# The end of a mixer: one conv tile before the reciprocal, output banks emptied between two roundings, attention tiles first

## The reference

```python
r = x + 0.5 * rms_norm(swiglu_ffn(rms_norm(x, norm_ffn1_pre), w_ffn1_gate_up, w_ffn1_down), norm_ffn1_post)
z = rms_norm(r, norm_mix_pre) @ w_in               # q | k | v | b | c | xv
attn_out = attend(q, k, v, attn_sinks)             # 8 heads, window of chunks of 64, 512 wide
conv_out = b * causal_conv3(c * xv)                # 512 wide
mixed = concat([rms_norm(attn_out, norm_attn_out), rms_norm(conv_out, norm_conv_out)]) @ w_out
r = r + rms_norm(mixed, norm_mix_post)
r = r + 0.5 * rms_norm(swiglu_ffn(rms_norm(r, norm_ffn2_pre), w_ffn2_gate_up, w_ffn2_down), norm_ffn2_post)
gate = sigmoid(rms_norm(r, norm_ple_pre) @ w_ple_gate)
r = r + rms_norm(gate * (p @ w_ple_proj), norm_ple_post)
```

## Time and profile before

| | |
|---|---|
| median of 3 runs | 1093.67 us (1092.20 to 1093.82) |
| the profiled execution's own time | 1093.74 us |
| its span | 1091.9 us |
| mean granted TensorE clock | 0.987 |
| TensorE busy | 1043.2 us (96%) |
| VectorE busy | 700.8 us (64%) |
| ScalarE busy | 509.6 us (47%) |
| GpSimd busy | 288.6 us (26%) |

### The profile page before, as it was taken

One profiled execution on the slowest core, in us unless ns is written; L12 is line 12 of the kernel. 1 busy time (PEld: TensorE's weight loads), 2 busy tenths in 40 slices (PEclk: granted clock), 3 DMA queues, 4 the chain that ended last, 5 costly groups with the idle time before them and its releaser, 6 DMA issues.

```text
span 1091.9 us, 20075 instructions
## 1 busy us (share of the span) xinstructions
PE 1043.2 (96%) x8095; PEld 1017.4 (93%) x8095; DVE 700.8 (64%) x1057; ACT 509.6 (47%) x927; POOL 288.6 (26%) x222
## 2 busy tenths in 40 slices
PE   5999999999999999999989899899999999999896
PEld 4999999999999998888979889899999999999796
DVE  5898777776511278577782889877777651127833
ACT  4545555555422254434453554555555542226653
POOL 4113443431211132000322411434343121113311
PEclk8999999999999999999989999999999999999999
DMA  7223342435323323213222221434243532333002
GB/s 221 67 71 88 106 117 79 115 94 144 100 64 102 77 46 98 56 46 79 59 59 79 78 77 40 111 84 116 81 113 100 138 106 62 99 97 94 25 1 83
DMA packets 182678, 94.76 MB, mean 87 GB/s; under 512 B 11768, under 2 KB 180928, under 8 KB 182592
## 3 DMA queue, kind: packets, MB, share of 16 engines
q1 hardware_dynamic: 182576, 93.56, 30.9%
q10 hardware_dynamic: 16, 0.00, 0.0%
HBM read 91.15 MB, written 2.50 MB: 86 GB/s over the span
## 4 chain that ended last, share of the span: by engine, by line
PE 77%; DVE 15%; ACT 3%; issue 2%; POOL 1%; DMA 1%; DVEq 0%; SPq 0%; ACTq 0%; POOLq 0%
PE bank L1640 12%; PE bank L1642 12%; PE bank L1641 12%; PE bank L1750 9%; PE bank L1753 9%; PE bank L1752 9%; PE bank L1675 3%; PE misc L1804 2%; PE misc L1750 2%; PE misc L1753 2%; PE misc L1752 2%; DVE w_split L1070 1%; DVE x_lo L1100 1%; DVE r L1091 1%; DVE w_up L1070 1%
## 5 line engine op out<-in xcount | busy, mean ns | idle before, releaser
L1642 PE MATMUL bank<-h_hi,w_split 128*128 128x272 f32 x704 | 203.8, 290 | 0.0
L1640 PE MATMUL bank<-h_hi,w_split 128*128 128x272 f32 x704 | 203.0, 288 | 0.0
L1641 PE MATMUL bank<-h_lo,w_split 128*128 128x272 f32 x704 | 202.2, 287 | 0.0
L1070 DVE TENSOR_TENSOR w_split<-raw,w_split 128x1408 fp32r<-128x1408 f32 (+2 forms) x66 | 98.2, 1500 | 154.1 <-ACT w_split L638 154.1
L570 POOL TENSOR_TENSOR ssq<-ssq,sq 128x272 f32<-128x272 f32 x112 | 108.5, 968 | 237.2 <-ACT sq L643 226.7
L1641 PEld LDWEIGHTS bank<-h_lo,w_split 128*128 128x128 f32 x704 | 132.6, 188 | 0.1
L1640 PEld LDWEIGHTS bank<-h_hi,w_split 128*128 128x128 f32 x704 | 132.4, 188 | 0.1
L1642 PEld LDWEIGHTS bank<-h_hi,w_split 128*128 128x128 f32 x704 | 132.3, 188 | 0.0
L1750 PE MATMUL bank<-t_hi,even_blocks 128*128 128x272 f32 x432 | 126.0, 292 | 6.6 <-issue 3.8
L1753 PE MATMUL bank<-t_hi,even_blocks 128*128 128x272 f32 x432 | 125.4, 290 | 0.0
L1752 PE MATMUL bank<-t_lo,even_blocks 128*128 128x272 f32 x432 | 124.8, 289 | 0.0
(11 more groups left out here) (243 smaller groups left out, 2628.4 us busy)
## 6 DMA issues: line engine op xcount, KB each, us to landing
raw_up<-w_ffn_gate_up SPq DMA_DIRECT2D x88, 512.0 KB, 4.9
raw<-w_ffn_down SPq DMA_DIRECT2D x32, 704.0 KB, 4.9
raw<-w_in SPq DMA_DIRECT2D x14, 512.0 KB, 4.3
raw<-w_ple_gate SPq DMA_DIRECT2D x8, 512.0 KB, 3.8
x_tok<-x_prompt SPq DMA_DIRECT2D x4, 512.0 KB, 5.3
raw<-w_in SPq DMA_DIRECT2D x8, 256.0 KB, 3.8
raw<-w_out SPq DMA_DIRECT2D x16, 128.0 KB, 3.4
raw<-w_out SPq DMA_DIRECT2D x8, 256.0 KB, 3.6
```

What stands on the lines that cost most here:

```text
L1070: nc.vector.tensor_tensor(chunk_part(c, 1), chunk_raw(c), chunk_part(c, 0).bitcast(F32), ALU.subtract).then_inc(lo_made, 1)
L1640: nc.tensor.matmul(psum(u), wh, hi, start=(k == 0), stop=False)
L1641: nc.tensor.matmul(psum(u), wh, lo, start=False, stop=False)
L1642: mm = nc.tensor.matmul(psum(u), wl, hi, start=False, stop=(k == n - 1))
```

## The change

Three things are written in another order; no instruction is added or taken away but for a register operation or so.

1. *The last tile of half A before the reciprocal.* On VectorE `mix_scale(0)` moves from unit 32 to unit 33, so that unit 33 (b3, half A) is evacuated ahead of it; `mix_los(0)` moves behind the split of weight chunks 2 and 3, and `mix_scale(3)` ahead of `mix_los(2)`. On ScalarE the squares of b2 and b3 come ahead of `mix_his(0)`, and the split of weight chunk 3 ahead of `mix_his(1)`.
2. *Banks emptied between the roundings.* On ScalarE both last roots come first, then banks 0 and 1 of out's half A are emptied, then `mix_his(2)`, then banks 2 and 3, then `mix_his(3)`.
3. *Attention tiles first.* On TensorE half B of out's first group runs tiles 0 to 3 for units 0 and 1, then for units 2 and 3, and only then tiles 4 to 7 for all four. In half A the sum of group 3 moves from tile 6 of the first pair to tile 4 of unit 2, and units 2 and 3 are made one after the other.

```diff
--- before.py
+++ after.py
@@ -959,30 +959,32 @@
                     mix_squares(2 * KA, 3 * KA)
                 if v == 32:
                     mix_root(0)
-                    mix_his(0)
                 if v == 33:
                     mix_squares(3 * KA, 3 * KA + 2)
+                    mix_his(0)
                 if v == 34:
                     mix_root(1)
                     split_hi(c0 + 20)
                     mix_squares(3 * KA + 2, 3 * KA + 3)
+                    split_hi(c0 + 21)
                 if v == 35:
                     mix_his(1)
                     mix_squares(3 * KA + 3, 3 * KA + 4)
-                    split_hi(c0 + 21)
             act.wait_ge(conv_turned, 1)
             nc.scalar.activation(conv_new[:], bT[0:4 * KA, 0:P], ACT.Copy).then_inc(conv_out, 1)
             mix_root(2)
-            mix_his(2)
             mix_root(3)
-            mix_his(3)
 
 
             def out_evacuate(i, h, m):
                 number = SQ0["out"] + (4 * h + m if i == 0 else 8 + OUT_SQUARES.index(("y", h, m)))
                 evacuate(U0["out"] + 8 * i + 4 * h + m, half(y_out, 4 * i + m, h), number)
 
-            group(C0["out"], lambda h, j: (out_evacuate(0, h, 2 * j), out_evacuate(0, h, 2 * j + 1)))
+            out_evacuate(0, A, 0), out_evacuate(0, A, 1)
+            mix_his(2)
+            out_evacuate(0, A, 2), out_evacuate(0, A, 3)
+            mix_his(3)
+            second_half(C0["out"], lambda h, j: (out_evacuate(0, h, 2 * j), out_evacuate(0, h, 2 * j + 1)))
             c1, squares = C0["out"] + 2 * SLOTS, SQ0["out"] + 8
             for m in range(4):
                 out_evacuate(1, A, m)
@@ -1545,19 +1547,15 @@
                     attention_out(d - 2)
                 if 0 <= d < NTASK:
                     softmax_scale(d)
-                if v == 32:
+                if v == 33:
                     mix_scale(0)
-                if v == 33:
-                    mix_los(0)
                 if v == 34:
                     mix_scale(1)
             split_lo(c0 + 20)
             split_lo(c0 + 21)
-            mix_los(1)
-            mix_scale(2)
-            mix_los(2)
-            mix_scale(3)
-            mix_los(3)
+            mix_los(0), mix_los(1)
+            mix_scale(2), mix_scale(3)
+            mix_los(2), mix_los(3)
 
 
             second_half(C0["out"])
@@ -1941,9 +1939,17 @@
                 i, h, pos = v // 8, v % 8 // 4, v % 4
                 if i == 0 and pos == 0:
                     units = [(U0["out"] + w, C0["out"] + w % 4, lambda w=w: out_ready(w)) for w in range(v, v + 4)]
-                    hooks = {6: lambda: all_sums(SUM0["mix"] + 3)} if h == A else {}
-                    hi_pass(units[0:2], m_high, h, lambda k: pe.wait_ge(m_hi_made, 8 * h + k + 1), hooks)
-                    hi_pass(units[2:4], m_high, h, lambda k: None)
+                    def arrived(k):
+                        pe.wait_ge(m_hi_made, 8 * h + k + 1)
+                    if h == A:
+                        hi_pass(units[0:2], m_high, A, arrived)
+                        hi_pass(units[2:3], m_high, A, lambda k: None, {4: lambda: all_sums(SUM0["mix"] + 3)})
+                        hi_pass(units[3:4], m_high, A, lambda k: None)
+                    else:
+
+                        hi_pass(units[0:2], m_high, B, arrived, {}, range(0, KA))
+                        hi_pass(units[2:4], m_high, B, lambda k: None, {}, range(0, KA))
+                        hi_pass(units, m_high, B, arrived, {}, range(KA, KD))
                     for n, (u, c, _) in enumerate(units):
                         lo_pass(u, c, lambda k, h: half(m_lo, k, h), h, None if n else lambda k: pe.wait_ge(
                             m_ready, 8 * h + k + 1))
```

## The result

The changed kernel takes 1086.82 us (median of 4 runs, 1085.66 to 1087.30) beside 1093.27 us for the kernel before (4 runs): ratio 0.9937, 95% interval 0.9925 to 0.9949. The profiled execution took 1087.30 us, of which 1085.5 are its span. Two later measurements of the same program gave ratios of 0.9928 (0.9914 to 0.9941) and 0.9924 (0.9910 to 0.9937).

A forecast was written before the change was run, and what follows sets the result against it. TensorE was taken as the bound (77% of the chain), losing 7.99 us to two waits and the low clock behind them. Less 7.99 plus a new wait of 0.3 gave -7.7, from 1093.74 to 1086.0 us, range 1084.5 to 1088.6.

The forecast's parts named there:

- First wait: TensorE at the sum ahead of unit 35: wait 2.89 us, slow sum 0.43, slow unit 35 1.23; 4.55 us back.
- New wait for the weights of unit 2: TensorE at units 2 and 3 of out's half A waits for chunk 2's low part: 0.3 us, between 0 and 1.2.
- Rival 1: VectorE's full queue makes chunk 2's low part 2.3 us late and the clock falls: gain 4.6, 1089.1 us; 8%.
- Second wait: TensorE ahead of out's half B, waiting for half A's banks to be emptied: 2.38 us back.
- High pass of B: Out's half B, 64 matmuls: 9.51 us after the clock's fall against 8.45 without; 1.06 us back.
- the rule weighed in the prediction: Full-clock matmul follows after N/2.4 + 2.5 ns, 115.8 ns for 272; would give about 9.3 us, 1084.7; not adopted.
- Moves along: Out's second column group and the second FFN, released by TensorE's units or slots they free, shift with the gain.
- rival 4: TensorE's gained time is spent waiting at the second FFN's entry for something that doesn't move: 1093.7 us; 4%.
- Rival 2: Only one wait goes, TensorE still standing in half A or B: 4.55 or 3.44 come back, 1089.2 to 1090.3; 7%.
- The third sum and the tiles first: Moved sum in half A: no wait, over 1 us unmoved; half B tiles first: no wait, else no margin.
- B's `m_hi`: ScalarE ends `m_hi` 3 at 566.7, the thirteenth being there at 565.4, so half B has no wait.
- Rival 3: Small waits keep the clock at 0.50 over the out stage's 192 matmuls: up to 24.4 us more, 1110; 3%.

The follow-up runs named there:

- the first experiment: Kernel before with only the mixer's end changed (half A's last tile and squares moved ahead): 1093.15 us, ratio 0.9995.
- all banks last: Changed kernel with ScalarE emptying all four banks of out's half A after both groups of `m_hi` again: 1092.52 us, ratio 0.9981.
- the first repeat: Changed kernel measured again, unedited: 1085.50 us beside 1093.81.
- the copies earlier: Changed kernel with VectorE's two copies to `conv_rows` ahead of the last mixer weight's low part: 1085.09 us, ratio 0.9923.

## Why the prediction was right

The forecast was 1086.0 us, within 1084.5 to 1088.6; the measured medians of the changed kernel are 1086.82, 1085.50 and 1085.87. By its steps:

- *First wait.* Forecast 4.55 us back. Measured from unit 33's last matmul to the start of the out projection: 11.36 before (543.43 to 554.79), 7.47 after (543.79 to 551.26), 3.89 back; this is the largest error of the sum. The wait itself went as worked out: square at 545.21, added by 546.50, asked at 547.54. What the walk missed is 0.50 us ahead of the transposition of `conv_rows` (543.79 to 544.41 instead of 543.43 to 543.56) and a first matmul of unit 35 that holds the next back by 0.2.
- *New wait for the weights of unit 2.* Forecast 0.3, measured none: the high pass of half A takes 8.69 us (551.26 to 559.95) against 8.71 before. Rival 1 did not happen.
- *Second wait.* Forecast 2.38, measured 2.49: A's low pass to the start of B is 6.43 before (563.50 to 569.93) and 3.94 after (559.95 to 563.89).
- *High pass of B.* Forecast 1.06, measured 1.50: 9.51 before, 8.01 after. I took 0.132 us a matmul, A's 8.45 us over 64, for B at full clock, and B's is 0.125. What I misread is A: its pace is 0.125 too, but the first matmul behind a sum holds the next one back by 0.2 us, as in unit 35, and A has two such places. The rows show it: 40 matmuls from 551.26 to 556.49 and 24 from 556.74 to 559.95 are 5.23 and 3.21 us, and less 0.2 each they are 0.126 and 0.125 a matmul. B has no sum in it. The page cited for the rule weighed in the prediction (the Trainium skill, "TensorE: Matmul & The Clock Gate", section "Back-to-back issue gap") gives that formula for an isolated matmul; the trace lies between its 0.116 and my 0.132.
- Sum: 3.89 + 0.02 + 2.49 + 1.50 = 7.90, against the 7.99 - 0.3 of the prediction. That the total is only 0.2 off is luck: the term of the first wait was 0.66 too high, those of the new wait, the second wait and the high pass were 0.3, 0.1 and 0.4 too low.
- *Moves along.* The rest behind the stretch does, but in the first profile it was 1.14 us longer than before (509.55 against 508.41), and the program came 0.36 later to unit 33. So the profiled execution is 6.44 us faster (1093.74 to 1087.30) and not 7.90. The three ratios of the changed kernel come to 6.9, 7.9 and 8.3 us of the time before, around the stretch's 7.90. This is not rival 4, in which nothing comes back.
- *Rival 2* (only one wait goes) did not happen, but the first experiment shows what would have made it true: the first part alone brings 0.17 us, as the wait moves to the next place. My terms for the two waits add only because both parts were made.
- *The third sum and the tiles first.* Both were carried as zeros with a price if left out: over 1 us for the sum (measured 1.46), and "no margin" for the pairs (measured 1.42). On B's `m_hi` I was optimistic: the last is done at 568.5 and not 566.7, since VectorE came 0.4 us later to the weight splits, and these and the scalings ran slower beside GpSimd's additions (last section). The room that the new order leaves absorbed it.
- *Rival 3* (low clock): 1.00 from 546 to 576. It did not happen.

## What to carry to other kernels

When two waits follow each other, ask what the second is bound by before the first is priced: here the other engines' queue set when half B could start, so one and the same edit that brings TensorE there earlier was worth 0.17 us, and 2.61 us once that queue had been put in another order. In a queue that runs in order, put the work that frees a buffer between two groups of the work that fills the next, as soon as the buffer's last reader allows; putting that order back on one engine, with all else kept, cost 6 to 7 us. And where the whole time scatters by more than the effect, measure between two fixed instructions of the profile: the stretch repeated within 0.01 us where the clock did not fall inside it.

## What the runs showed of the hardware

**VectorE and GpSimd hold each other up.** With GpSimd's addition at 543.03 beside it, VectorE's pair of copies of 128x8 took 0.82 us and ended, by the start of the next row at 544.27, when the addition did (543.03 + 1.23 = 544.26); without it 0.24. The addition took 1.23 to 1.38 beside VectorE's work between SBUF tiles and 0.77 or 0.78 without. Four scalings at 565.78 took 2.07, with the second of the two additions in the row from 564.89 beside them, and 1.50 in the kernel before, with none. The Trainium skill, "SBUF — State Buffer", section "Who interferes with whom", says that the two engines share a pair of ports, that a copy can take it for a whole instruction and that an instruction with two inputs in SBUF meets GpSimd's reads. The traces agree: the first of the two copies was held for 0.58 us, and the reciprocal at 563.90, whose input is in PSUM, kept its 1.84 beside the addition at 564.89.

**The clock after a wait is not the same twice.** A wait of 2.7 or 2.3 us was followed by some 3 us at 0.50; that of 4.2 us in the first experiment by some 3, and that of 4.1 us with all banks last by about 6. The wait of 3.5 us in the second FFN was followed by none, some 3 or nearly 7 us at 0.50 in different executions of programs that are the same there; around that of 1.97 us ahead of the sum of squares behind the output projection (608.69 in the first profile of the changed kernel) it was none in the first repeat, some 3 us in the first profile, and nearly 7 with the copies earlier. The rest behind the stretch differs by 2.5 us over the twelve profiles, and the head of the program, where unit 33 was reached between 541.77 and 543.99, by 2.2. Three executions of the unedited changed kernel alone differ by 1.2 us in the rest and 1.0 in the head. Not all of it was traced to the clock.
